# Attention in a streaming encoder layer: score pieces of two heads alternate within a pair of heads

## What is computed

```python
logits = jnp.einsum('btgrd,btkgd->btgrk', qg, kg).astype(jnp.float32) * (A_HEAD_DIM ** -0.5)
dist = jnp.abs(q_pos[None, :, None] - sel).astype(jnp.float32)
logits = logits - slopes[None, None, :, :, None] * dist[:, :, None, None, :]
logits = jnp.where(valid[:, :, None, None, :], logits, -jnp.inf)
prob = jax.nn.softmax(logits, axis=-1).astype(v.dtype)
out = jnp.einsum('btgrk,btkgd->btgrd', prob, vg)
```

## Time and profile before

| what | value |
|---|---|
| median of three executions | 2789.45 us (2788.71 to 2790.51) |
| profiled execution | 2790.49 us |
| its span, first to last instruction | 2788.7 us |
| PE busy over the span | 2671.0 us, 96% |
| DVE busy | 2057.8 us, 74% |
| ACT busy | 1418.4 us, 51% |
| POOL busy | 1249.8 us, 45% |
| mean granted TensorE clock | 0.989 |

### The profile page before, as it was taken

The page is one execution under the profiler, slowest core; times in us unless marked ns, Lnnn a source line. Parts: engine busy times, 40 slices in busy tenths (PEclk is TensorE's granted clock), DMA queues, the critical chain, the costliest instruction groups (busy, mean ns, idle before and its releaser), DMA issues. The chain is left out here.

```text
span 2788.7 us, 40014 instructions
## 1 busy us (share of the span) xinstructions
PE 2671.0 (96%) x14029; PEld 2472.3 (89%) x14029; DVE 2057.8 (74%) x4123; ACT 1418.4 (51%) x2425; POOL 1249.8 (45%) x846
## 2 busy tenths in 40 slices
PE   6999999999999999999999789999989998999998
PEld 6999999999999999999998667777779997888886
DVE  6477899999999999851634678999976557555554
ACT  5377588776777778753222477777730011211111
POOL 1100288686878778883445374221354442111110
PEclk9999999999999999999999899999999999999999
DMA  4433323232433232243654632221165555122211
GB/s 171 123 119 122 126 93 125 94 124 99 141 104 115 83 127 98 90 131 122 198 172 135 174 104 85 63 66 46 47 244 167 187 165 176 50 73 74 66 57 39
DMA packets 271430, 320.35 MB, mean 115 GB/s; under 512 B 36609, under 2 KB 234753, under 8 KB 270589
## 3 DMA queue, kind: packets, MB, share of 16 engines
q1 hardware_dynamic: 170691, 189.97, 22.2%
q10 hardware_dynamic: 100538, 127.82, 13.1%
HBM read 196.36 MB, written 120.73 MB: 114 GB/s over the span
## 5 line engine op out<-in xcount | busy, mean ns | idle before, releaser
L1659 PE MATMUL psum<-hT_hi,j_whi 128*128 128x416 f32 x2440 | 871.1, 357 | 2.7 <-issue 2.7
L1659 PE MATMUL psum<-hT_hi,j_wlo 128*128 128x416 f32 x2440 | 858.1, 352 | 0.0
L1659 PE MATMUL psum<-hT_lo,j_whi 128*128 128x416 f32 x2440 | 857.0, 351 | 0.0
L1273 POOL TENSOR_TENSOR v_y<-v_y,v_product 128x422 f32<-128x422 f32 x459 | 557.4, 1251 | 89.4 <-ACT v_product L1255 89.3
L448 DVE TENSOR_SCALAR_CACHE_REDUCE s_tie<-s_key,s_bits 128x640 bf16<-128x640 f32 (+14 forms) x352 | 464.3, 1319 | 12.3
L1659 PEld LDWEIGHTS psum<-hT_hi,j_whi 128*128 128x128 f32 x2440 | 459.9, 188 | 12.5 <-issue 4.9
L1659 PEld LDWEIGHTS psum<-hT_lo,j_whi 128*128 128x128 f32 x2440 | 461.1, 189 | 9.4 <-issue 1.8
L1659 PEld LDWEIGHTS psum<-hT_hi,j_wlo 128*128 128x128 f32 x2440 | 459.7, 188 | 5.7
L1255 ACT ACTIVATE v_product<-v_x,v_taps 128x422 f32<-128x422 f32 x510 | 302.8, 641 | 84.4 <-POOL v_y L1273 60.7
L1521 ACT ACTIVATE j_out<-psum 128x416 f32<-128x416 f32 x285 | 144.7, 509 | 341.3 <-PE psum L1659 330.1
L1468 POOL TENSOR_TENSOR j_wlo<-j_w,j_whi 128x1024 fp32r<-128x1024 f32 x61 | 150.3, 2463 | 340.4 <-ACT j_whi L1503 340.2
(11 more groups left out here) (294 smaller groups left out, 4884.6 us busy)
## 6 DMA issues: line engine op xcount, KB each, us to landing
T_dram<-j_out ACTq DMA_DIRECT2D x59, 624.0 KB, 2.9
j_w<-in_w_in ACTq DMA_DIRECT2D x59, 512.0 KB, 3.7
m_gate<-T_dram SPq DMA_DIRECT2D x60, 416.0 KB, 3.5
T_dram<-j_out ACTq DMA_DIRECT2D x59, 416.0 KB, 2.4
m_oraw<-B_dram SPq DMA_DIRECT2D x15, 832.0 KB, 5.5
M_dram<-m_merged ACTq DMA_DIRECT2D x5, 1664.0 KB, 7.5
n_x<-in_x_prompt SPq DMA_DIRECT2D x16, 512.0 KB, 5.3
f_mraw<-M_dram SPq DMA_DIRECT2D x16, 512.0 KB, 4.7
```

The source lines that it names most:

```text
L1273: pool.tensor_tensor(y[k % 2][:], y[k % 2][:], product[n % RING][:], ALU.add).then_inc(added, 1)
L1659: last = pe.matmul(bank, w[p][:, k, :], h[:, k, t0:t0 + SPAN], start=(k == 0 and q == 0), stop=(k == KD - 1 and q == 2))
```

## The change

The list of score pieces of a group is made in another order. Before, all pieces of one head come one after the other. After, the heads of a group form two pairs, and within a pair the pieces alternate: piece 0 of the first head, piece 0 of the second, piece 1 of the first, and so on. The number of pieces, their sizes and the slots that they fall in stay. The look-up of the previous piece of a head goes through a dictionary. Banks and semaphore counts follow the new order. Since an exponential is placed behind the last piece of its head, its slot follows from the new order as well. For a group whose keys fit one piece the order stays as it was.

```diff
--- before.py
+++ after.py
@@ -1899,10 +1899,12 @@
     for group in groups:
 
         group.units = []
-        for h in group.heads:
+        for pair in (group.heads[0:2], group.heads[2:4]):
             for s, (a, w) in enumerate(parts(group.keys)):
-                group.units.append((h, s, a, w, units % QK, units // QK, units))
-                units += 1
+                for h in pair:
+                    group.units.append((h, s, a, w, units % QK, units // QK, units))
+                    units += 1
+        group.unit_of = {unit[0:2]: unit for unit in group.units}
 
         group.tiles = []
         for kt in range(-(-group.keys // P)):
@@ -2276,7 +2278,7 @@
             if s == 1 and h == 0 and group is GUARDED:
                 vec.wait_ge(late_ready, len(late_splits))
             if s:
-                _, _, _, _, previous, uses_of_bank, _ = group.units[(h - 4 * group.g) * len(parts(group.keys)) + s - 1]
+                _, _, _, _, previous, uses_of_bank, _ = group.unit_of[h, s - 1]
                 vec.wait_ge(qk_read[previous], uses_of_bank + 1)
             vec.wait_ge(qk_full, n + 1)
             vec.sem_inc(mark, 1)
```

## The result

Over 13 executions of each kernel the median is 2797.09 us after the change and 2790.48 before. The ratio is 1.0027, with a 95% interval of 1.0016 to 1.0038: slower by 0.27%, where +0.29% was forecast. The medians lie 6.6 us apart in the first series and 7.6 in the second.

A forecast was written before the change was run, and what follows sets the result against it. PE was taken as the bound, busy 96% of the span, with its waits for DVE and ACT in the attention deciding. Terms -8 - 1 - 3 + 20 - 2 + 2 = +8 us gave 2797.5 us, range 2786 to 2808.

The forecast's parts named there:

- Dependent neighbours cost DVE 0.3 us, independent ones nothing: DVE's 512-column pieces: dependent ones start 0.98 us apart, independent ones 0.68, so a dependent pair costs some 0.3 us.
- Gain 12 us: PE's waits in the attention: removing DVE's 79 own waits saves 12 us in all, bounds 5 and 17.8.
- The 8 us: From 1723 us on, PE's 7.9 us of waits for low parts, nearly all before a group's first `weigh`, counted as gone.
- The 1 us for banks: From 1723 us on, half of PE's 2.3 us of waits for banks counted as gone.
- The 3 us ahead of 1723: Attention before 1723 us, mostly short groups: 3 us of PE's waits saved, bounds 0 and 4.9.
- Delay of the last exponential, 20 us at 18 group ends: Group ends 15 to 32: third exponential directly ahead of the last on ACT delays it, making PE wait 20 us more.
- -2 for `a_kslo`: Groups 20 to 23: PE's 4.7 us wait for `a_kslo` absorbs 2 us of the delay, between 0 and 4.7.
- +2 for the middle pairs: Mid-group, two exponentials in adjacent slots make ACT's copy late; 2 us reach PE over all groups, between -2 and +8.
- The sum: Whole kernel: -8 - 1 - 3 + 20 - 2 + 2 = +8 us, giving 2797.5 us, +0.29%; forecast's chance 0.40.
- half the delay hidden: Group ends: only half of the 20 us delay is paid, about -2 us; within the faster rival, chance 0.12.
- 8 for the middle: Rival, mid-group: late copies delay low part, next piece and bank, +8 us more in some 16 groups, 2805; chance 0.15.
- Marks set in advance: Signs for the profile after: PE's and DVE's waits and attention's end; wrong if PE's exponential waits stay below some 18 us.

The follow-up runs named there:

- e1: Kernel before with only DVE's wait for its own previous piece removed, leaving head minimum and right softmax out; 2778.35 us, ratio 0.9959.
- e2: Kernel before, pieces in old order with their waits, only the exponentials moved to the slots of alternating pairs; 2804.88 us, ratio 1.0056.
- e6: Changed kernel, but only the third and fourth head of a group alternate; 2802.11 us, ratio 1.0041 against the kernel before.
- e9: Changed kernel with every group's third head's exponential cut to its first 128 columns, its softmax left out; 2774.54 us, ratio 0.9946 against the kernel before.
- e10: Kernel before with the third head's exponential cut to 128 columns, its softmax left out; 2785.25 us, ratio 0.9990.
- e5: Changed kernel, but only the first pair of heads alternates, third and fourth go one after the other; 2782.19 us, ratio 0.9976 against the kernel before.
- e3: Changed kernel, but only a group's first four pieces alternate between its first two heads, the rest head by head; 2779.14 us, ratio 0.9964 against the kernel before.
- e4: The changed kernel once more, unchanged, for its time and a second profile; 2796.73 us, ratio 1.0028 against the kernel before.

## Why the prediction was right

The time, the sign and the mechanism hold: removed waits are worth some 11 us, the delayed last exponential costs more. Several terms of the sum were off in ways that cancelled. By its own steps:

- **Dependent neighbours cost DVE 0.3 us, independent ones nothing.** Right: pieces that read `a_lows` start 0.97 us apart before and 0.67 after. The rule of the Trainium skill ("VectorE: DVE Perf Modes", "The DRAIN you can't avoid"), measured there on copies, that a semaphore after each operation costs nothing extra, does not hold for this instruction.
- **Gain 12 us.** Measured 10.7 (e1), but the terms differ. The 8 us were for low parts from 1723 us on, where the wait fell by 5.6 in e1 (7.9 to 2.3). The 1 us for banks there was a rise of 1.2 (2.3 to 3.5). The 3 us ahead of 1723 were 4.2 (low parts 7.8 to 5.2, banks 12.1 to 10.5). 2.3 us came at `a_kslo` (4.7 to 2.4), where no gain had been counted. That the total is near 12 is partly luck.
- **Delay of the last exponential, 20 us at 18 group ends.** The mechanism is shown from three sides: alone it gives the loss (e2), the second pair alone has it (e6), a short third exponential removes it (e9 against e10). The size was somewhat too large: PE's wait grew by 17.5 us, the moved exponentials alone cost 15.8, and beside the removal they cost 17 to 18 (6.6 or 7.6, and 10.7).
- **-2 for `a_kslo`**, because part of the delay would be absorbed there. The wait did fall by 1.9 (4.7 to 2.8), but not for this reason: with the delay alone (e2) it is 4.4, with the removal alone (e1) 2.4. The size was right by luck.
- **+2 for the middle pairs.** PE's waits for banks from 1723 us on rose from 2.3 to 5.1, of which e1 alone has 1.2. So some 1.6 us go to the moved exponentials, of the forecast size; e5 against e3 (2.6 us) is within the noise.
- **The sum** was +8, the measurement +6.6 and +7.6. Both large terms were too large, by 1 and by 2 to 4 us, and these errors partly cancelled; the sum is better than its terms. The ends of the range do not follow from the terms named for them: half the delay hidden gives -12 + 10 - 2 + 2 = -2, and a gain of 5 with 8 for the middle gives -5 + 20 - 2 + 8 = +21, not +18.
- **Marks set in advance.** PE's wait for exponentials "at 25 us or more": 27.0 and 26.4, but in 25 places and not in over 30. Its wait for low parts "below 8": 7.5 in one profile, 8.8 in the other. The attention was to be about 8 us longer: 9.8 and 5.2. DVE's wait for copies past 35 us, with PE's waits for banks growing too, was named as a sign of being wrong. The first part came true (47.8), the second only in the long groups: 2.3 to 5.1 us there, 14.4 to 13.7 over the whole attention. Both the removal (32.6 us in e1) and the moved exponentials (37.7 in e2) make DVE stand longer for copies, and little of it reaches PE.

## What to carry to other kernels

When a list of work is reordered, look at everything that is placed by the last item of a head, row or tile: here two exponentials of up to 2 us moved together on an engine that had little to do with the change, which cost 16 us where the removed waits gave 11. A wait is worth removing where the other engine stands behind it. Alternating only four pieces (e3, ratio 0.9964) removes 50 of the 79 waits, nearly all of those at the group ends, and leaves the last two exponentials where they were, and it gives 10 us where the full alternation loses 7. A distance such as `AHEAD` is counted in slots of the order, but two queues may stand at different slots at the same time; one slot less cost 50 to 60 us.

## What was not expected

The granted clock at the start of the attention differs from one execution to the next, and with it the time at which the long groups begin. The window from 40 to 80 us behind the first score matmul (busy us of PE, PEld, DVE, ACT, POOL, then the clock) in the first profile of the changed kernel:

```profile
1612.30:1652.30 40.00, 31.98 (x164) 26.41 (x162) 31.45 (x94) 28.09 (x64) 31.86 (x29) 0.87 0.40 108
```

and in the second (e4):

```profile
1603.20:1643.20 40.00, 30.79 (x185) 24.75 (x183) 34.05 (x98) 31.38 (x72) 35.61 (x31) 1.00 0.44 118
```

The same program did 164 matmuls at a clock of 0.87 in one and 185 at 1.00 in the other (167 of the kernel before at 0.96). 0.87 of 2.4 GHz as a mean says that PE was for part of the time at the lower of its two levels; both profiles had 0.77 in the 40 us before, where PE was busy for 29.8 and 30.5 of 40 us.

The turn of the cached keys in group 20 divides the attention. Times from the first score matmul to this turn, and from it to the start of the last `weigh`, with the clock from 40 to 80 us:

| kernel | to the turn, us | from the turn, us | clock |
|---|---|---|---|
| before | 229.9 | 254.4 | 0.96 |
| changed, first profile | 229.6 | 264.5 | 0.87 |
| changed, second profile (e4) | 223.7 | 265.9 | 1.00 |
| e1, removal alone | 227.1 | 246.7 | 0.91 |
| e2, exponentials moved | 229.5 | 269.9 | 0.96 |
| e3, four pieces | 222.2 | 250.7 | 0.96 |
| e6, second pair | 230.5 | 266.4 | 0.96 |
| e9, third short | 219.3 | 250.5 | 1.00 |
| e10, its control | 227.9 | 253.0 | 0.96 |

Behind the turn the two profiles of the changed kernel agree within 1.4 us: there the change costs 10 to 11.5 us. Ahead of it they differ by 5.9 us, so how much the short groups gained by the change, where I had forecast 3 us, cannot be told from one profile: it is between 0 and 6 us with the clock mixed in. That it is more than nothing is made likely by e3, which has the clock of before in this window and comes to the turn 7.7 us earlier. What lets the clock rise sooner in one run was not tried and stays open.
